# Scaling the attention probabilities in their own iteration

## What is computed

```python
z = h @ w_in                       # 1024 -> 4096: q, k, v, u, two gates
y_na = neighbourhood_attention(q, k, v, rpb) @ w_na_out
y_f = fourier_mix(uf) @ w_f_out
return (sigmoid(ga + b0) * y_na + sigmoid(gf + b1) * y_f) @ w_o
```

```python
s = einsum(q, k_win) * scale + bias          # masked outside the window
p = softmax(s)                               # exp(s - max) / sum
o = einsum(p, v_win)
```

## Time and profile before

| | |
|---|---|
| median of three runs | 1647.44 us (1645.39 to 1648.55) |
| the profiled execution's own time | 1645.68 us |
| its span in the trace | 1643.9 us, 20426 instructions |
| TensorE clock granted over the span | 0.998 of full speed |
| HBM read | 304.00 MB, 187 GB/s over the span |

### The profile page before, as it was taken

How to read it: one execution, slowest core, us unless ns; L and a number is a source line. 1 busy time by engine, 2 the same in 40 slices (tenths; PEclk the granted TensorE clock), 3 DMA queues, 4 the chain that set the end, 5 groups by cost and what they waited for, 6 DMA issues and landing times.

```text
span 1643.9 us, 20426 instructions
## 1 busy us (share of the span) xinstructions
PE 1620.8 (99%) x7578; PEld 1336.8 (81%) x7578; DVE 942.1 (57%) x948; ACT 789.9 (48%) x945; POOL 134.5 (8%) x197
## 2 busy tenths in 40 slices
PE   9999999999999999999899999999999999999998
PEld 7888877788888888888678888888888888888887
DVE  6454655575454744555557545477755457774455
ACT  6443444544444544445454534466544445664444
POOL 1001210011000000111100000031100002110000
PEclk9999999999999999999999999999999999999999
DMA  8777554447565567765435575553666565266562
GB/s 281 251 215 227 187 186 136 151 157 228 191 199 184 169 223 211 228 213 191 137 127 181 192 242 177 194 177 108 193 204 201 182 198 177 75 216 198 176 205 89
DMA packets 212275, 307.23 MB, mean 187 GB/s; under 512 B 12708, under 2 KB 155448, under 8 KB 212216
## 3 DMA queue, kind: packets, MB, share of 16 engines
q1 hardware_dynamic: 210792, 304.07, 56.7%
q0 software_dynamic: 1120, 1.86, 0.5%
q10 hardware_dynamic: 304, 0.50, 0.1%
HBM read 304.00 MB, written 2.88 MB: 187 GB/s over the span
## 4 chain that ended last, share of the span: by engine, by line
PE 94%; ACT 3%; DVE 2%; issue 2%; POOLq 0%; POOL 0%; DVEq 0%; ACTq 0%
PE pg L1942 20%; PE pg L1944 19%; PE pg L1943 19%; PE acc L1942 9%; PE acc L1944 9%; PE acc L1943 9%; PE pg L2061 2%; ACT whi L934 1%; PE pg L1955 1%; DVE work L1571 0%; PE acc L2336 0%; PE acc L2294 0%; PE acc L2153 0%; PE pg L2336 0%; DVE wlo L1349 0%
## 5 line engine op out<-in xcount | busy, mean ns | idle before, releaser
L1349 DVE TENSOR_TENSOR wlo<-raw,whi 128x2048 fp32r<-128x2048 f32 (+1 forms) x267 | 610.8, 2288 | 479.8 <-ACT whi L934 479.6
L934 ACT ACTIVATE whi<-raw 128x2048 fp32r<-128x2048 f32 (+1 forms) x267 | 509.6, 1910 | 325.2 <-PE pg L1944 154.5
L1942 PE MATMUL pg<-whi,xTh 128*128 128x512 f32 (+1 forms) x1456 | 576.8, 396 | 0.1
L1944 PE MATMUL pg<-whi,xTl 128*128 128x512 f32 (+1 forms) x1456 | 567.2, 390 | 0.0
L1943 PE MATMUL pg<-wlo,xTh 128*128 128x512 f32 (+1 forms) x1456 | 566.4, 389 | 0.0
L1942 PEld LDWEIGHTS pg<-whi,xTh 128*128 128x128 f32 x1456 | 274.1, 188 | 57.7 <-DVE xTl L1364 1.4
L1944 PEld LDWEIGHTS pg<-whi,xTl 128*128 128x128 f32 x1456 | 273.7, 188 | 56.7
L1943 PEld LDWEIGHTS pg<-wlo,xTh 128*128 128x128 f32 x1456 | 274.2, 188 | 54.9 <-issue 1.0
L1942 PE MATMUL acc<-whi,bTh 128*128 128x512 f32 (+1 forms) x572 | 228.4, 399 | 0.0
L1944 PE MATMUL acc<-whi,bTl 128*128 128x512 f32 (+1 forms) x572 | 222.8, 390 | 0.0
L1943 PE MATMUL acc<-wlo,bTh 128*128 128x512 f32 (+1 forms) x572 | 221.8, 388 | 0.0
(11 more groups left out here) (246 smaller groups left out, 1063.4 us busy)
## 6 DMA issues: line engine op xcount, KB each, us to landing
raw<-in_ffn_w_in SPq DMA_DIRECT2D x172, 512.0 KB, 4.7
raw<-in_ffn_w_out SPq DMA_DIRECT2D x88, 512.0 KB, 4.2
raw<-in_w_gate_up SPq DMA_DIRECT2D x88, 512.0 KB, 4.6
raw<-in_mix_w_in SPq DMA_DIRECT2D x64, 512.0 KB, 4.4
raw<-in_w_down SPq DMA_DIRECT2D x44, 512.0 KB, 4.0
raw<-in_w_in SPq DMA_DIRECT2D x24, 512.0 KB, 4.6
raw<-in_mix_w_o SPq DMA_DIRECT2D x16, 512.0 KB, 4.5
raw<-in_w_o SPq DMA_DIRECT2D x16, 512.0 KB, 4.5
```

The source lines that it names most:

```text
L934: act_e.activation(whi[:, slot, 0:cols], raw[:, slot, 0:cols], ACT.Copy).then_inc(s.w_hi_ready, 1)
L1349: v.tensor_tensor(wlo[:, slot, 0:cols], raw[:, slot, 0:cols], f32(whi[:, slot, 0:cols]), ALU.subtract)\
L1942: pe.matmul(dst, xh, wh, start=first and i == 0, stop=False)
L1944: mm = pe.matmul(dst, xl, wh, start=False, stop=last and i == len(pairs) - 1)
```

## The change

DVE's call of `scale` moves. Before, iteration i scaled pair i - 1, behind the low part of unit i + 8 and ahead of the gate bias and of pair i's maximum. Now iteration i scales its own pair i as its last step, behind the maximum and the Fourier part's low half. The same instructions with the same waits are issued; no other engine's program changes.

```diff
                     if i < 9:
                         refills(i + 8)
-                    if 1 <= i <= 8:
-                        scale(i - 1)
                     if i >= 2:
                         add_gate_bias((i - 2) // 2, i % 2)
                     if i < 8:
                         softmax_max(i)
                     if i in channels:
                         g = channels.index(i)
                         v.wait_ge(s.fT_hi, 4 * l + g + 1)
                         v.tensor_tensor(fTl[:, g, :], acc[1][:, 0:T], f32(fTh[:, g, :]), ALU.subtract).then_inc(s.fT_lo, 1)
+                    if i < 8:
+                        scale(i)
```

## The result

The changed kernel takes 1628.11 us (median of four runs, 1628.06 to 1628.24) against 1647.43 before (median of four as well, 1645.39 to 1648.55): a ratio of 0.9884, with a 95% interval of 0.9867 to 0.9901. The forecast was 1630.6, and faster at 0.92. The sign, the place and the mechanism were right; the gain was 19.3 us where 16.8 were forecast.

A forecast was written before the change was run, and what follows sets the result against it. PE bounds the kernel, busy 1620.8 of 1643.9 us. Waits of 15.2 plus clock of 1.6 give 16.8 us, so 1647.44 - 16.8 = 1630.6; own range 1627.5 to 1633.5, for all cases 1627 to 1637.

The forecast's parts named there:

- The bound and the mechanism: PE bounds the kernel; its transposes wait for scaling queued on DVE behind a low part, 12 times, 14.5 us together.
- Term 1: PE's 12 waits for DVE's second scaling piece in both mixers all go: 15.2 us.
- Term 2: Lowered PE clock in iteration 2, behind the 3.68 us wait, no longer occurs: 1.6 us, bounds 0 to 3.2.
- The clock's cause: In iteration 2, an idle TensorE falls to the half clock, at a moment varying between runs; 1.6 us in the profile.
- Pair 1 beside POOL: Pair 1's scaling multiplications enter POOL's sums: 0.42 and 0.22 us at the median, 1.29 and 1.28 at their longest; no cost.
- the 1.8 us of the rival: POOL's contention holds DVE, so PE waits 0.9 us in iteration 2, 1.8 in two layers; within a 0.13 chance.
- The other spares: Time left before PE wants moved results: pair 0 2.6 us, pair 1 1.5 to 3.4, output behind pair 5's scaling 1.8.
- The values: Value transfers for attend(0) land 2.0 us after issue, at 246.8, before PE wants them at 249.4: zero cost.
- The rival of a new wait in iteration 2: Late values (2.2 us), POOL contention (1.8) or both (4.0) make PE wait: 1632.4 to 1634.6, chance 0.13.
- a gain given back: Something downstream, such as the weights, runs by its own time; all but some 2 us return: 1644 to 1647, chance 0.04.
- The rival of a slower kernel: Low parts queue behind late exponentials; at 10 us late PE loses 2.5 in each of 8 iterations: 1650.6, chance 0.03.
- the forecast's own range: Whole kernel, 1627.5 to 1633.5 us: clock term 0 to 3.2 instead of 1.6, and 1.5 for the runs' spread.

The follow-up runs named there:

- the filled stop: Kernel before the change, with 14 unread 512-column matmuls added in iteration 1 of each mixer between scores and transposes: 1644.59 us, ratio 0.9979.
- the kernel with eight more maxima: Changed kernel with eight maxima that nobody reads added to every scaling: 1647.44 us, ratio 1.0002.

## Why the prediction was right, and by how much off

*The bound and the mechanism.* Right. The scaled probabilities were ready and stood in DVE's queue behind a low part that waits for PE's progress. The chain from `scale` to the transposes is gone, and moving it ahead of the low part in either place gives the same time.

*Term 1, 15.2 us.* The second mixer, where the profile of before shows a clock of 1.00, went from 69.16 to 61.28 us: 7.88, so 15.8 for both against 15.2. Of the rest 0.09 in each is the transposes' start, 0.54 behind the scores when nothing is late where I had taken 0.63 from another instruction, and iteration 4's transposes had been 0.09 late without a row that says so (272.50 behind an edge product at 271.99).

*Term 2, 1.6 us.* This is the term that was mis-sized. In the profiled execution it was right: the first mixer lost 9.46 us, 1.58 more than the second. But I bounded a fall of the clock by the one that the profile shows, 1.6 us, and two by 3.2. The kernel with pairs 1 to 7 moved shows 2.5 us at either stop, and its two mixers are 6.6 and 6.7 us longer than the changed kernel's 61.28, of which 3.8 are the stop itself; some 2.8 us are then the clock, from the transposes on. Two such falls make 5.6 us, from 1643.9 (1628.1 and twice 7.88) to 1649.5; the slowest run seen of the kernel before is 1649.83.

*From the profiled execution to the median.* Here lay the error in kind. I carried the 1.76 us by which the median stood above the profiled time over to the changed kernel as if they belonged to every kernel. They were the same clock loss, more of it in the median run. After the change the profiled time is the median's, within 0.01 us. The kernel before, in its 15 runs beside the last experiments, took 1645.8 us at a mean clock of 0.998, 1646.9 to 1647.2 at 0.997, 1648.1 to 1648.6 at 0.996 and 1648.8 to 1649.8 at 0.995. Its spread was a finding, not noise: 19.3 us = 15.8 of waiting and, as the rest, some 3.5 of clock.

*The clock's cause.* Right, and now shown by the filled stop. The Trainium skill (TensorE: Matmul & The Clock Gate, Part 1: The HAM clock gate) has it that an idle TensorE falls to the half clock and that the moment varies. The traces agree: behind the same idle time of 3.68 us the granted clock was 0.76, 1.00, 0.67 and 0.66 over four windows.

*Pair 1 beside POOL.* The price was within the bounds: 0.69 and 0.76 us, between the median's 0.42 and 0.22 and the 1.29 and 1.28 of pair 0 before. POOL paid too: its sums end at 252.13 where they ended at 250.26, and nobody waited for it. Nearly all of that is one operation beside unit 10's low part (DVE, 247.35 to 249.64), and not beside the scaling. The first row is that operation, the second another of the same size:

```profile
247.41 2.29 POOL L813 TENSOR_TENSOR work<-work 128x2 f32<-128x2 f32 x1
...
251.93 0.20 POOL L813 TENSOR_TENSOR work<-work 128x2 f32<-128x2 f32 x1
```

The rule that speaks of contention with VectorE holds in kind (Trainium skill, GPSIMD Engine Reference, 8. Key points); its cost on the path was zero, not the 1.8 us of the rival.

*The other spares.* Pair 0: 2.6 forecast, 2.6 read. Pair 1: 1.5 to 3.4 forecast, 2.6 read. The output's low half: 1.8 forecast, 2.1 read. The values: the 2.0 us taken for the landing was right. The rival of a new wait in iteration 2 therefore did not occur, and neither did a gain given back: the stretch between the mixers is 467.8 us before and after. The rival of a slower kernel put its point of decision at 7.5 us of lateness and looked only at PE's wait for the low part. No run tests that number: the kernel with eight more maxima lost the whole gain at 3.2 us a pair by waits for the scaling and the output's low half, and none for a low part in the mixers. Exponentials that come late would hold up the scaling in the same way, which the rival left out; no run made them late.

*The sums.* They come out, but for the upper end of the forecast's own range: 1630.6 + 1.6 + 1.5 is 1633.7 and not 1633.5. Nothing hangs on it.

## What to carry to other kernels

In an in-order queue, an instruction whose data are ready should not stand behind one that waits for the engine being fed; look for a wait of the bound engine whose releaser had its inputs long before. Waits found that way can't be subtracted one by one, since a long stop hides the ones that come behind it: recompute each due time with the stop gone, or move all of them. And when a kernel's runs spread and its granted clock varies, take the profiled execution and the median apart before carrying a difference over.

## What the runs showed of the hardware

Filling the long stop of TensorE in either mixer with 14 useless matmuls made the kernel 3.8 us faster, with the wait as it was. Stops of about 1 us, six of them in the kernel before, were followed by a full clock; those of 3.68 us were not always. In the kernel with eight more maxima a stop of 1.49 us was followed by a full clock once and by a fallen one once, which cost 1.65 us.

An unused tile of 32 bytes per partition, ahead of the tables and the work area, cost 1.7 us in the parts of the kernel that have nothing to do with it (0.4 ahead of the first mixer, 0.5 between them, 0.85 behind), and one of 64 bytes at most 0.6. Which instructions are slower was not found.
